# Recurrence of a hybrid trunk on one core: solution and transposed values placed beside the products of levels 1 and 2

## The chip, the cores and the metric

The kernel runs on one core of one Trainium2 chip. The metric is the device time of one execution in microseconds; three runs of a kernel are summed up by their median. TensorE is called PE here, its weight loads PEld, VectorE DVE and ScalarE ACT. PSUM is used as eight banks of 128 partitions by 512 float32 values, `bank0` to `bank7`.

## The reference, cut to what matters

The kernel computes two layers of a trunk over 256 tokens and 256 context tokens: a token mixer (windowed attention, a bidirectional RWKV-7 recurrence, differential attention), then a dense feed-forward layer or a mixture of experts. The change touches the recurrence alone, which a scan defines, per head, over a state of 64 by 64:

```python
def rwkv_scan(s0, r, w, k, v, a_vec, b_vec, reverse, emit):
    def step(s, inp):
        r_t, w_t, k_t, v_t, a_t, b_t = inp
        sa = jnp.einsum('bhvk,bhk->bhv', s, a_t)
        s = s * w_t[:, :, None, :] + sa[..., None] * b_t[:, :, None, :] + v_t[..., None] * k_t[:, :, None, :]
        y = jnp.einsum('bhvk,bhk->bhv', s, r_t) if emit else None
        return s, y
...
    for d, reverse in enumerate((False, True)):
        w_c, k_c, a_c = dirs_c[d]
        s_ctx, y_c = rwkv_scan(s0, r_c, w_c, k_c, v_c, -kk_c, kk_c * a_c, reverse, need_ctx)
        w_l, k_l, a_l = dirs_l[d]
        _, y_l = rwkv_scan(s_ctx, r_l, w_l, k_l, v_l, -kk_l, kk_l * a_l, reverse, True)
```

There are 8 heads of 64 values, two directions and 512 steps (context, then tokens). In layer 1 the context's outputs are not needed (`need_ctx` is false there).

## The kernel before

The 512 steps of a layer are worked off in 8 chunks (`NCH`) of 64 steps. Within a chunk all 64 steps are solved together: a triangular 64 by 64 system for each of 16 head-directions, named by `q` (0 to 7) and `h` (0 or 1, the upper or lower half of the partitions). A step on all sixteen is sixteen small products of 64 by 64 (`pair(x, q, h)` cuts the block out of a 128 by 512 tile). The product's rows are those of the operands' partitions, its columns those of the output's partitions, so one product uses a quarter of the array.

The inverse of the triangular matrix is doubled in five rounds, n = 0 to 4:

- `level(i, n)` multiplies the strictly lower part with the inverse so far, sixteen products into `level_bank` (bank 6). DVE multiplies them by a mask into `T1` (`masked`, L2437, one instruction of 128x512).
- `inverse_doubled(i, n)` waits for `T1` and makes both the grown inverse (`grown`, bank 0) and its transpose (`grown_turned`, bank 1), 32 products, for n = 4 the transpose alone. ACT copies the two banks to `X[1]` and `XT[1]` (`copied`, L1627); the next level waits for the first copy.

Around these stand, in chunk i: `from_state(i)` (the right-hand side: L923 and L927 from the state, then `narrow`, L818), `solve(i - 1)` (the solution U of the chunk before, banks 2 and 7, partitions 0 to 63), `y_of_chunk` and `state` (both L818, both read the copied solution and the kept products), `values_turned(i)` (the values transposed by an identity, banks 2 and 7, partitions 64 to 127), `bonus` (one product of 128x512, for i up to 4), and four pairs `against(i, n)` (four products of 64x192 each), which DVE multiplies by a mask into `PB` (`kept`, L2456). `level(i, 3)` and `level(i, 4)` carry another sixteen products each of the next chunk's matrices (`gram`), one for one between their own (`beside`). In layer 1 no output is made for chunks 0 to 3, so `y_of_chunk` is empty there.

Each engine works off its own list in the order of the code; nothing is scheduled. Lists meet in semaphores: `A` (banks read by ACT), `V_` (banks 3 to 5, read by DVE, claimed in turn), `S` (banks 6 and 7, read by DVE). `pe.wait_ge(A.free, ...)` waits until ACT has copied a bank out, `pe.wait_ge(S.free, ...)` until DVE has masked it. A `V_` claim waits until DVE is through with the bank claimed three claims earlier.

The order of PE in a chunk i from 1 on is: level 0, solve, doubled 0, y, level 1, state, doubled 1, values, bonus, level 2, against 0, doubled 2, against 2, level 3 with gram, against 4, doubled 3, against 6, level 4 with gram, from_state, doubled 4. DVE's list in the same chunk: masked 0, `rates_in` and `operands` of chunk i + 1 (L2402 to L2413), masked 1, `emitted` (L2464), `responses` (L2418), `state` (L2470 to L2480), `bonus_out` (L2367), masked 2, kept 0 and 1, `centre` (L2389), `bonus_keys` (L2354 and L2355, for i under 4), kept 2 and 3, masked 3, kept 4 and 5, `begin_inverse` (L2441), kept 6 and 7, masked 4, `begin_turned` (L2446, L2448), `bonus_in` (L2361, L2362).

## Time and profile before

| | |
|---|---|
| median of 3 runs | 2892.83 us (2891.24 to 2895.13) |
| profiled execution, its own time | 2893.22 us |
| its span (first to last instruction) | 2891.4 us |
| PE busy | 2797.3 us, 97% of the span, 29030 matmul records |
| DVE busy | 1185.1 us, 41% |
| ACT busy | 683.0 us, 24% |
| recurrence of layer 0, chunk 0 level 3 to the last chunk | 177.1 to 343.1 us |
| recurrence of layer 1, the same | 1440.3 to 1603.3 us |
| mean granted PE clock | 0.991 |

A float32 product shows as two matmul records and two weight loads, so that sixteen products are written x32. In the timeline a row's second number runs from its first start to the modelled end of its last matmul. In a dense run the next step starts a little before that end; the distance from start to start is what a step takes. The two stretches of the recurrence are 329 us of the 2891.

### The profile page before, as it was taken

The numbers are of one execution on the slowest core, as the hardware profiler recorded it, in microseconds if no ns is written. First come the engines' busy times: TensorE is split into PE (matmuls) and PEld (weight loads), VectorE is DVE, ScalarE is ACT, GpSimd is POOL, SyncE is SP. The second block draws the span as 40 slices with busy tenths as digits, with TensorE's granted clock in tenths as the row PEclk, the third lists the DMA queues.
The fourth block names the chain that finished last, engine by engine and source line by source line (L and its number), as shares of the span: only waits on it lengthen the run. The fifth ranks groups of instructions, "written<-read, shape, count | busy, mean of one in ns | idle before, by whom it ended". The sixth has DMA issues, their size and how long they took to land.

```text
span 2891.4 us, 63725 instructions
## 1 busy us (share of the span) xinstructions
PE 2797.3 (97%) x29030; PEld 1683.3 (58%) x29030; DVE 1185.1 (41%) x2444; ACT 683.0 (24%) x1425; POOL 3.0 (0%) x7
## 2 busy tenths in 40 slices
PE   7999999999999999999999999989999999999997
PEld 4478777445777888864588787863333333333332
DVE  4777565445545444247786564431111011011101
ACT  2345312544322111013454126520000000000000
POOL 0000000000000000000000000000000000000000
PEclk9999999999999999999999999999999999999999
DMA  7100143212242433232000442459999999999995
...
DMA packets 188787, 534.55 MB, mean 185 GB/s; under 512 B 6113, under 2 KB 80097, under 8 KB 171105
## 3 DMA queue, kind: packets, MB, share of 16 engines
...
## 4 chain that ended last, share of the span: by engine, by line
PE 92%; DVE 4%; ACT 1%; SPq 1%; issue 1%; DMA 1%; DVEq 0%; ACTq 0%
PE bank L572 68%; PE bank L700 12%; PE bank L1337 8%; PE bank L818 2%; PE bank L1199 1%; SPq L2990 1%; DVE WR L2456 1%; ACT ar L1627 0%; DMA rep<-in_repeated 0%; PE bank L923 0%; ACT WR L1627 0%; DVE RS L2330 0%; DVE AT L2127 0%; DVE ar L2389 0%; DVE WR L2437 0%
## 5 line engine op out<-in xcount | busy, mean ns | idle before, releaser
L572 PE MATMUL bank<-AT,WR 128*128 128x512 f32 (+1 forms) x1408 | 521.4, 521 | 5.9 <-ACT AT L1627 3.7
L1627 ACT ACTIVATE ar<-bank 128x256 f32<-128x256 f32 (+2 forms) x338 | 155.1, 463 | 1535.3 <-PE bank L572 1028.3
L572 PE MATMUL bank<-WR,ar 128*32 128x512 f32 (+1 forms) x4464 | 444.5, 555 | 1.6 <-DVE ar L2899 1.6
L572 PE MATMUL bank<-ar 128*32 128x512 f32 (+6 forms) x3990 | 429.6, 509 | 9.9 <-ACT ar L1627 5.9
L572 PEld LDWEIGHTS bank<-AT,WR 128*128 128x128 f32 x1408 | 263.0, 192 | 213.0 <-issue 196.9
L572 PEld LDWEIGHTS bank<-ar 128*32 128x32 f32 (+3 forms) x3990 | 176.1, 124 | 248.5 <-issue 237.3
L572 PEld LDWEIGHTS bank<-WR,ar 128*32 128x32 f32 x4464 | 143.7, 110 | 288.4 <-issue 285.8
L1627 ACT ACTIVATE WR<-bank 128x512 f32<-128x512 f32 (+1 forms) x224 | 122.8, 592 | 200.0 <-PE bank L572 174.7
L572 PE MATMUL bank<-AT,ar 128*32 128x512 f32 (+1 forms) x1456 | 151.5, 561 | 11.3 <-ACT AT L1627 11.3
L2909 DVE TENSOR_TENSOR YB<-YB,bank 128x512 f32<-128x512 f32 x28 | 18.0, 684 | 342.9 <-PE bank L572 342.9
L2917 DVE TENSOR_TENSOR ar<-ar,bank 128x512 f32<-128x512 f32 (+1 forms) x48 | 29.8, 621 | 286.9 <-PE bank L572 285.5
L1627 ACT ACT_TABLE_LOAD x111 | 142.4, 1283 | 14.3 <-DVE ar L2291 8.5
L572 PE MATMUL bank<-WR 64*64 64x64 f32 x5120 | 113.7, 221 | 3.7 <-issue 1.7
L572 PEld LDWEIGHTS bank<-WR 64*64 64x64 f32 x5120 | 100.7, 134 | 18.4 <-DVE WR L2437 7.9
L572 PEld LDWEIGHTS bank<-AT,ar 128*32 128x32 f32 x1456 | 47.8, 110 | 105.8 <-issue 103.6
L572 PE MATMUL bank<-WR,HT 64*64 64x64 f32 x2560 | 94.7, 221 | 5.6 <-ACT WR L1627 3.1
L572 PEld LDWEIGHTS bank<-WR,HT 64*64 64x64 f32 x2560 | 82.7, 134 | 26.5 <-ACT WR L1627 16.7
L2437 DVE TENSOR_TENSOR WR<-bank,tab 128x512 f32<-128x512 f32 x80 | 55.2, 690 | 60.0 <-PE bank L572 58.4
L1627 ACT ACTIVATE ar<-ar 128x256 f32<-128x256 f32 (+2 forms) x137 | 54.1, 446 | 103.3 <-DVE ar L2839 35.3
L1337 PE MATMUL bank<-AT,WR 128*128 128x256 f32 x320 | 76.1, 381 | 0.0
L700 PE MATMUL bank<-ar,WR 128*128 128x256 f32 x336 | 75.0, 379 | 0.6 <-issue 0.6
L700 PE MATMUL bank<-ar 128*128 128x256 f32 x328 | 73.1, 379 | 0.0
...
## 6 DMA issues: line engine op xcount, KB each, us to landing
...
```

What stands on the lines that cost most here:

```text
L572: return pe.matmul(o, lhsT, rhs, start=first, stop=last)
L700: last = pe.matmul(out, one, two, start=not opened and k == 0, stop=k == h.K - 1, skip_group_check=opened)
L818: last = pe.matmul(pair(bank, q, 1 - h if crossed else h), lhs(q, h), rhs(q, h), start=not (opened or (more and q)), stop=not more, skip_g ...
L1199: last = pe.transpose(bank[:, 128 * b:128 * b + 128], Pb[:, n % 2, c, 128 * b:128 * b + 128], eye)
L1337: last = pe.matmul(out, lhs(k), rhs(k), start=not opened and k == 0, stop=k == 3, skip_group_check=opened)
L1627: return act.activation(out, in_, func, **k)
L2437: TT(dq(T1), step_product(banks[6]), mk(M_LEVEL + 1 + n), ALU.mult).then_inc(S.free, 1)
L2456: TT(PB[:, q:q + 2, h, :], bank[:, 0:384].rearrange("p (q w) -> p q w", q=2), stacked[:, q // 4, :].unsqueeze(1).to_broadcast([128, 2, 192 ...
L2909: TT(x, x, b3, ALU.add).then_inc(S.free, 1)
L2917: TT(x, x, bank[:, 0:WIDE[s_]], ALU.mult).then_inc(up.free, 1)
L2990: sp.dma_start(tab[:, TAB_FIRST:], io["tables"][:, TAB_FIRST:]).then_inc(tables_in, 16)
```

## The change

What it does, by engine:

- PE: `solve(i - 1)` is no longer a step of its own; its sixteen products are placed between those of `level(i, 1)`. `values_turned(i)` is likewise placed between those of `level(i, 2)`. `y_of_chunk(i - 1)` and `state(i - 1)` stand behind `inverse_doubled(i, 1)`. `inverse_doubled(i, 2)` stands ahead of `against(i, 0)`, and each further pair of `against` one place later, the last one between level 4 and `from_state`. The number of products is the same.
- PSUM: the level's product, the grown inverse and its transpose take turns over banks 0, 1 and 6 (`level_bank`, `grown_bank`, `turned_bank`); the solution lies in bank 2 and the transposed values in bank 7, each over all 128 partitions. From this come new waits: level 0 for the copy of the right-hand side (`G`), doubled 0 for the copy of the last transpose (`XT`, which for n = 4 goes to a third tile), `from_state` for the copy of `XT` of round 3.
- ACT: the solution is copied behind the two copies of round 0 instead of ahead of them; the two copies of a pair wait once.
- DVE: `responses` and `centre` stand behind masked 1, `emitted` ahead of masked 2, `state` and `bonus_out` behind masked 2, `kept` one place later each, the last pair behind masked 4, and `bonus_keys` behind kept 4 and 5, ahead of masked 4.

The mask is one 128x512 instruction for each level, as before.

The diff, cut to its core:

```diff
+        def level_bank(i, n):
+            return banks[(0, 1, 6)[(5 * i + n + 1) % 3]]
+        def grown_bank(i, n):
+            return banks[(0, 1, 6)[(5 * i + n + 2) % 3]]
+        def turned_bank(i, n):
+            return banks[(0, 1, 6)[(5 * i + n) % 3]]
+        solved_bank, gram_bank = banks[2], banks[7]
...
-                grown, grown_turned, level_bank, gram_bank = banks[0], banks[1], banks[6], banks[7]
-                two = (banks[2], banks[7])
...
+                def value_turned(i, q, h):
+                    c = CH * (i if q < 4 else BWD[i])
+                    last = mm(pair(gram_bank, q, h), Rv[64 * h:64 * h + 64, q % 4, c:c + CH],
+                              eye[64 * h:64 * h + 64, 64 * h:64 * h + 64], True, True)
...
+                def solve(i, q, h):
+                    last = mm(pair(solved_bank, q, 1 - h), pair(XT[2], q, 1 - h), pair(G, q, 1 - h), True, True)
...
                     for q in range(8):
+                        bank = level_bank(i, n)
                         for h in range(2):
...
+                        for h in range(2 if beside else 0):
+                            if beside == "solve":
+                                solve(i - 1, q, h)
+                            elif beside == "values":
+                                value_turned(i, q, h)
...
                     if i:
                         level(i, 0)
-                        solve(i - 1)
                         inverse_doubled(i, 0)
+                        level(i, 1, "solve")
+                        inverse_doubled(i, 1)
                         y_of_chunk(i - 1, ybank)
-                        level(i, 1)
                         state(i - 1)
-                        inverse_doubled(i, 1)
-                        values_turned(i)
+                        level(i, 2, "values")
                         if i <= 4:
                             bonus(i - 1)
-                        level(i, 2)
+                        inverse_doubled(i, 2)
                         pe.wait_ge(responses_ready, seen(responses_ready))
                         against(i, 0)
-                        inverse_doubled(i, 2)
-                        against(i, 2)
                     level(i, 3, "X" if i < NCH - 1 else None)
-                    against(i, 4)
+                    against(i, 2 if i else 4)
                     inverse_doubled(i, 3)
-                    against(i, 6)
+                    against(i, 4 if i else 6)
                     level(i, 4, "LT" if i < NCH - 1 else None)
-                    if i == 0:
+                    if i:
+                        against(i, 6)
+                    else:
                         pe.wait_ge(uv_cleared, seen(uv_cleared))
                     ybank = from_state(i)
                     inverse_doubled(i, 4)
```

On PE, in chunk 1 of layer 0, these rows stood ahead of the change (`WR,HT` is a level's product, `WR` alone a doubling or the solution, L818 the `narrow` steps, `tab,ar` the values, `ar,tab` the bonus, `HT,RS 128x192` an `against`):

```order
L572 MATMUL bank<-WR,HT 64x64 x16
L572 MATMUL bank<-WR 64x64 x48
L818 MATMUL bank<-WR 64x64 x16
L572 MATMUL bank<-WR,HT 64x64 x16
L818 MATMUL bank<-WR 64x64 x16
L572 MATMUL bank<-WR 64x64 x32
L572 MATMUL bank<-tab,ar 64x64 x16
L572 MATMUL bank<-ar,tab 128x512
L572 MATMUL bank<-WR,HT 64x64 x16
L572 MATMUL bank<-HT,RS 128x192 x4
L572 MATMUL bank<-WR 64x64 x32
L572 MATMUL bank<-HT,RS 128x192 x4
```

With the change the same place reads (L583 is L572 there, L829 is L818; the pairs of x2 rows go on eight times each):

```order
L583 MATMUL bank<-WR,HT 64x64 x16
L583 MATMUL bank<-WR 64x64 x32
L583 MATMUL bank<-WR,HT 64x64 x2
L583 MATMUL bank<-WR 64x64 x2
...
L583 MATMUL bank<-WR 64x64 x34
L829 MATMUL bank<-WR 64x64 x32
L583 MATMUL bank<-WR,HT 64x64 x2
L583 MATMUL bank<-tab,ar 64x64 x2
...
L583 MATMUL bank<-ar,tab 128x512
L583 MATMUL bank<-WR 64x64 x32
L583 MATMUL bank<-HT,RS 128x192 x4
```

The solution and the values have no rows of sixteen of their own any more. Behind level 0 stands doubled 0 at once, behind it level 1, and behind that doubled 1; the two L818 steps are together; level 2 is followed by the bonus alone.

On DVE, in chunk 1 of layer 0, from masked 2 to masked 4 (L2437 the mask, L2456 `kept`, L2354 and L2355 `bonus_keys`):

```order
L2437 TENSOR_TENSOR WR<-bank,tab 128x512
L2456 TENSOR_TENSOR WR<-bank,tab 128x2x192 x2
L2389 TENSOR_TENSOR ar<-ar 128x520
L2354 TENSOR_TENSOR ar<-ar 128x512
L2355 TENSOR_SCALAR ar<-ar,vec,cvec 128x512
L2456 TENSOR_TENSOR WR<-bank,tab 128x2x192 x2
L2437 TENSOR_TENSOR WR<-bank,tab 128x512
L2456 TENSOR_TENSOR WR<-bank,tab 128x2x192 x2
L2441 COPY_PREDICATED WR<-tab,bank 128x512
L2456 TENSOR_TENSOR WR<-bank,tab 128x2x192 x2
L2437 TENSOR_TENSOR WR<-bank,tab 128x512
```

With the change (L2455 is the mask, L2474 `kept`, L2372 and L2373 `bonus_keys`), from masked 3 on:

```order
L2455 TENSOR_TENSOR WR<-bank,tab 128x512
L2474 TENSOR_TENSOR WR<-bank,tab 128x2x192 x2
L2459 COPY_PREDICATED WR<-tab,bank 128x512
L2474 TENSOR_TENSOR WR<-bank,tab 128x2x192 x2
L2372 TENSOR_TENSOR ar<-ar 128x512
L2373 TENSOR_SCALAR ar<-ar,vec,cvec 128x512
L2455 TENSOR_TENSOR WR<-bank,tab 128x512
L2474 TENSOR_TENSOR WR<-bank,tab 128x2x192 x2
L2464 COPY_PREDICATED HT<-tab,bank 128x512
```

The two instructions of `bonus_keys` moved from ahead of masked 3 to ahead of masked 4, and the last pair of `kept` moved behind masked 4.

## Rows read from the trace of the kernel before

**Rows 1.** The page: busy time, share of the span and instructions

```profile
PE 2797.3 (97%) x29030; PEld 1683.3 (58%) x29030; DVE 1185.1 (41%) x2444; ACT 683.0 (24%) x1425; POOL 3.0 (0%) x7
```

**Rows 2.** Busy us by stretch, both recurrences: PE, PEld, DVE, ACT, POOL, PE clock, DMA

```profile
177.08:343.09 166.01, 157.94 (x5528) 138.45 (x5526) 120.50 (x212) 82.67 (x204) 0.00 (x0) 1.00 0.02 5
1440.33:1603.30 162.97, 152.03 (x5304) 134.13 (x5302) 117.91 (x204) 82.53 (x204) 0.00 (x0) 1.00 0.02 4
```

**Rows 3.** Timeline of PE, chunk 1 of layer 0: start, length, instruction

```profile
183.65 0.97 PE L572 MATMUL bank<-WR,HT 64*64 64x64 f32 x26
...
184.59 2.33 PE L572 MATMUL bank<-WR 64*64 64x64 f32 x94
186.85 1.15 PE L818 MATMUL bank<-WR 128*64 128x64 f32 x32
```

**Rows 4.** Timeline of PE, chunk 4 of layer 0, values and bonus to level 3

```profile
262.84 1.10 PE L572 MATMUL bank<-tab,ar 64*64 64x64 f32 x32
263.87 1.12 PE L572 MATMUL bank<-ar,tab 128*128 128x512 f32 x2
...
268.81 0.27 PE L572 MATMUL bank<-WR,HT 64*64 64x64 f32 x2
...
269.90 0.92 PE L572 MATMUL bank<-HT,ar 64*128 64x192 f32 x8
```

**Rows 5.** Timeline of PE, chunk 2 of layer 0, level 2 to against 4

```profile
217.82 1.15 PE L572 MATMUL bank<-WR,HT 64*64 64x64 f32 x32
218.90 0.92 PE L572 MATMUL bank<-HT,ar 64*128 64x192 f32 x8
219.76 1.16 PE L572 MATMUL bank<-WR 64*64 64x64 f32 x64
220.85 0.92 PE L572 MATMUL bank<-HT,ar 64*128 64x192 f32 x8
...
223.28 0.92 PE L572 MATMUL bank<-HT,ar 64*128 64x192 f32 x8 [0.41 <-DVE WR L2456]
```

**Rows 6.** Timeline of DVE over the same stretch

```profile
219.01 0.69 DVE L2437 TENSOR_TENSOR WR<-bank,tab 128x512 f32<-128x512 f32 x1 [0.40 <-PE bank L572]
...
221.40 0.68 DVE L2354 TENSOR_TENSOR ar<-ar 128x512 f32<-128x512 f32 x1
222.12 0.55 DVE L2355 TENSOR_SCALAR ar<-ar,vec,cvec 128x512 f32<-128x512 f32 x1
222.58 1.02 DVE L2456 TENSOR_TENSOR WR<-bank,tab 128x384 f32<-128x384 f32 x2
```

**Rows 7.** Timeline of PE, chunk 3 of layer 1, where y is empty

```profile
1495.22 1.15 PE L572 MATMUL bank<-WR,HT 64*64 64x64 f32 x32 [0.78 <-ACT WR L1627]
1496.30 1.15 PE L818 MATMUL bank<-WR 128*64 128x64 f32 x32
```

**Rows 8.** Who waited for whom: PE, layer 0, us in total, times, longest

```profile
PE bank L572 <- issue: 2.4, 7, 0.4
PE bank L927 <- issue: 1.7, 3, 0.7
...
PE bank L818 <- issue: 1.0, 2, 0.7
PE bank L923 <- issue: 0.3, 1, 0.3
PE bank L818 <- ACT WR L1627: 0.2, 1, 0.2
```

**Rows 9.** The same, layer 1

```profile
PE bank L572 <- issue: 4.0, 9, 0.9
...
PE bank L818 <- issue: 2.2, 3, 1.1
```

**Rows 10.** Busy time by stretch, from one issue gap of PE to the next

```profile
212.24:215.98 3.74, 3.31 (x128) 3.04 (x127) 2.82 (x7) 0.73 (x2) 0.00 (x0) 1.00 0.03 7
235.88:239.61 3.73, 3.36 (x127) 3.09 (x128) 2.57 (x6) 0.44 (x1) 0.00 (x0) 1.00 0.02 4
```

145 lines of the change are left out of this document (78 added, 67 removed).

## The prediction

> **What bounds the kernel now.** I read the page's busy shares first: TensorE is busy for 2797.3 of 2891.4 us, VectorE for 41% and ScalarE for 24% [rows 1]. So only what lengthens or shortens TensorE's own list counts. The change touches two stretches, so the busy time by stretch comes next [rows 2]: 166.01 us in layer 0 and 162.97 us in layer 1, with PE busy for 157.94 and 152.03 us. DVE and ACT have a quarter and half of the time free there, and the granted clock is 1.00, its upper level. The stretches hold seven chunks with changed order each, and chunk 0, which keeps its order. Then the timelines of PE and DVE, for one thing: how long a step of sixteen products takes, and what covers the time between a product and the step that needs it masked or copied. Last the waits, for what is idle on PE already: mostly "issue", a wait that no other engine ends [rows 8, 9].
>
> Steps, from start to start. A level alone takes 1495.22 to 1496.30, 1.08 us [rows 7]; y and state have as many products and I give them the same. Level 0, solution and doubled 0 take 183.65 to 186.85, 3.20 us, of which a doubling is 1.09 (219.76 to 220.85), so that level 0 and solution have about 1.05 each [rows 3, 5]. The values take 262.84 to 263.87, 1.03, and I count 1.0 since the last of them runs into the bonus [rows 4]. Thirty-two products placed one for one, level 3 with gram, take 268.81 to 269.90, 1.09 us, no more than sixteen alone [rows 4]. An against takes 218.90 to 219.76, 0.86 us [rows 5].
>
> **What goes.** In each of 14 chunks the solution's 1.05 and the values' 1.0, together 2.05 us, since level 1 with the solution and level 2 with the values should take the 1.09 of level 3 with gram: each uses the same two quarters of the array beside the level's two. That is 28.7 us off PE's list. Of PE's order it is the only gain; no DMA is issued in the moved steps, and no queue of SP or POOL is passed.
>
> **What it uncovers.** Those steps were cover.
> (a) Doubled 0 now stands right behind level 0. A level started at 217.82, its mask on DVE ran from 219.01 for 0.69 us, the doubling started at 219.76 [rows 5, 6]: 1.94 us after the level's start, of which the level's step is 1.08. Idle: 0.86 us.
> (b) Level 1 stands right behind doubled 0 and needs the copy of the grown inverse. In layer 1, chunks 1 to 4, y is empty and this wait is there today: 0.78 us by the row [rows 7], 0.85 from start to start. Idle: 0.85 us, but new only in the ten chunks that had y there.
> (c) Doubled 1 stands right behind level 1, where the state step was: 0.86 us. `operands` and `rates_in` stand ahead of this mask on DVE; they take some 3.1 us behind masked 0, and level 1 now ends 3.1 us after masked 0's end too, so I add nothing.
> (d) Doubled 2 stands behind the bonus (1.05 us, cover enough) in chunks 1 to 4, and bare in chunks 5 to 7: 0.86 us there. Its old cover, against 0, now covers the copy ahead of level 3, which needs 0.85 of its 0.86.
> (e) The last `kept` pair stands behind masked 4, and `narrow` in `from_state` waits for it. From the end of level 4: against 6 (0.86) and the state part (0.97) give PE 1.83 us; DVE begins the pair when against 6 is over and takes 1.02 for it [rows 6], so it is ready at about 2.05. Idle 0.2 us in chunks 4 to 7. In chunks 1 to 3 `bonus_keys` (0.68 and 0.55, 1.2 together [rows 6]) stand ahead of masked 4 and start only behind kept 4 and 5; mask and last pair come about 0.9 later: 1.1 us.
> (f) Given back: today `bonus_keys` delay kept 2 and 3, and against 4 waits for a bank, idle 0.41 [rows 5], 0.62 more than a normal start; it starts behind doubled 3 now. Minus 0.62 in chunks 1 to 3. y's wait for the copied solution, 0.2 us once by its row [rows 8] and some hundredths elsewhere, goes: minus 0.1 in the ten chunks with y.
> (g) The rotated banks: level 0 waits for the copy of G, which has all of doubled 4 (1.08) for some 0.8; doubled 0 for the last XT, which has level 0. Nothing, while doubled 4 stands there; bare it would be 0.8. State and bonus_out on DVE run later, but their readers, `from_state` and against 2, are over 1 us away: nothing. The copy of U stands behind two copies on ACT and y comes a doubling later: nothing.
>
> The sum per chunk. Layer 0, chunks 1 to 3: -2.05 + 0.86 + 0.85 + 0.86 + 1.1 - 0.62 - 0.1 = +0.9, three times 2.7. Chunk 4: -2.05 + 2.57 + 0.2 - 0.1 = +0.6. Chunks 5 to 7: 0.86 more, +1.5, three times 4.5. Layer 1, chunks 1 to 3: -2.05 + 1.72 + 1.1 - 0.62 = +0.15, together 0.45. Chunk 4: -0.1. Chunks 5 to 7: 4.5. In all +12.6 us: by waits alone the change is a loss.
>
> **What the idle time is worth.** PE is short of instructions in the same stretches. Its issue waits are 2.4 + 1.7 + 1.0 + 0.3 = 5.4 us in 13 pieces in layer 0 and 4.0 + 2.2 = 6.2 us in 12 pieces in layer 1 [rows 8, 9]. Idle time is counted from the end of the last matmul, some 0.22 us behind its start, and a normal start follows after 0.03, so each piece costs 0.19 more: 11.6 + 25 x 0.19 = 16.4 us. From one such gap to the next lie 256 records (128 matmuls and 127 or 128 loads) and 3.7 us [rows 10]. I read this as a fetch of 256 instructions that takes about 3.65 us, begun when the one before is begun upon. In layer 0 there are 5528 + 5526 records, 43 blocks, 3.84 us each, 3.64 without the idle pieces: right at that bound. The new order spreads the same records over more time, so waits for a mask and for a fetch fall together. Where can fetches still bind? From level 1 to the end of doubled 2: 128 + 128 + 64 + 64 + 4 + 128 + 128 = 644 records, 2.5 blocks, 9.1 us, in 1.95 + 1.09 + 1.08 + 1.08 + 1.09 + 1.05 + 1.09 = 8.4 us. Up to 0.7 us a chunk is lost there, and I take 0.57, since a block seldom begins just there: 14 times, 8.0 us. Elsewhere a chunk has 14 us for 900 records, which need 12.8. So 16.4 - 8.0 = 8.4 us come back. Bounds: nothing, or all 16.4.
>
> Net +12.6 - 8.4 = +4.2 us on the profiled execution's 2893.22, of which the span is 2891.4. It lies 0.4 us above the median of 2892.83, so I put the median at 2897.
>
> A rule of the Trainium skill speaks against the paired steps. The rows have 64 matmul records in 1.09 us, 17 ns each [rows 4]. "TensorE: Matmul & The Clock Gate", section "Wait — 56ns, not 53.3ns?", says that starts never follow closer than about 25 ns, however small the product; by it an estimate of a paired step is 64 x 25 ns = 1.6 us, and the sum would be 28 x 0.5 = 14 us worse. The trace does not agree: in separate quarters of the array starts are 17 ns apart. By the row it is +4.2, by the rule +18.
>
> **The rivals.**
> 1. The issue waits stay as they are (slower). Mechanism: gaps fall at fixed counts of instructions, and if these counts fall inside the dense run level 1 to doubled 2, a gap there delays mask and copy with it and nothing is absorbed. For it: today's gaps sit in runs just as dense. Against it: 3.84 us a block becomes about 3.9, above the 3.65. Price: +12.6, 2905.4. It decides from the point where less than 6.8 of the 16.4 come back. Chance 0.26.
> 2. The waits overlap more than I sum (faster). The last `kept` pair has work ahead of it on PE; if `narrow` never waits, (e) falls away, 6 x 1.1 + 8 x 0.2 = 8.2 us, and with 13 of the 16.4 back it is +12.6 - 8.2 - 13 = -8.6, 2884. For it: DVE is idle for a quarter of the stretch. Against it: masked 4 cannot be earlier than level 4, and the pair is behind it. Chance 0.14.
> 3. The paired steps cost more than 1.09, because the solution reads two tiles that ACT wrote last or because of their starts: 28 x 0.5 = +14 us on +4.2, 2911. Against it: all of today's pairs are at 1.09 [rows 4]. Chance 0.03.
>
> **How the numbers follow.** Forecast, a loss in waits mostly paid by fetches that are hidden: 0.57, 2897, its own range 2890 to 2901. Rival 1 0.26, rival 2 0.14, rival 3 0.03. A difference of 0.2%, 5.8 us, is about what a measurement of this kernel can tell from no change: same means 2887.0 to 2898.6. Of the forecast's 0.57 some 0.07 lies over 2898.6; of rival 1 0.05 and of rival 2 0.04 lie within. Same 0.59, slower 0.31, faster 0.10. The range reaches from 2887 to 2906: it leaves out rival 3, the rest of rival 1 above its price, and most of rival 2.
>
> **What would show it.** In the changed profile, both stretches a little longer, near 168 and 165 us. PE waits for DVE's mask (L2455) ahead of doubled 0 and doubled 1, 28 times some 0.6 to 0.7 by the rows, and in six chunks ahead of doubled 2; for ACT's copy ahead of level 1 in all 14; for `kept` (L2474) ahead of `narrow`, near 0.9 in the six chunks with `bonus_keys`. Paired steps at 1.09. PE's issue waits down from 11.6 to about 5 us. The forecast is wrong if issue waits stay near 11 (then rival 1), if the waits for `kept` are missing (rival 2), or if the median moves without these stretches moving: a longer list of instructions that shifts fetch gaps elsewhere.

## The result, and the profile after

| | before | after |
|---|---|---|
| median | 2892.71 us (2891.24 to 2895.13) | 2919.03 us (2917.68 to 2922.07) |
| profiled execution, its own time | 2893.22 us | 2918.77 us |
| its span | 2891.4 us | 2916.9 us |

The ratio is 1.0091, with a 95% interval of 1.0078 to 1.0103: slower by 26 us, clear of the noise, and outside the predicted range of 2887 to 2906. The direction of the net forecast (+4.2) was right, the size was not.

Where did it come from? The stretches are cut here from the mask of chunk 0, level 3, to the last mask of chunk 7. Busy time by stretch; the columns are those of [rows 2]. Before:

```profile
177.08:340.01 162.93, 154.86 (x5418) 135.61 (x5420) 119.81 (x212) 82.08 (x203) 0.00 (x0) 1.00 0.02 5
1440.33:1600.29 159.96, 149.02 (x5194) 131.36 (x5196) 117.22 (x204) 81.93 (x203) 0.00 (x0) 1.00 0.02 4
```

And after:

```profile
175.77:352.41 176.64, 150.33 (x5394) 130.59 (x5394) 119.12 (x209) 83.81 (x203) 0.00 (x0) 0.94 0.02 4
1452.71:1624.57 171.86, 139.62 (x5170) 120.27 (x5169) 116.09 (x201) 83.81 (x203) 0.00 (x0) 0.99 0.02 4
```

The two stretches grew from 322.89 to 348.50 us, by 25.6; the span grew by 25.5. So all of it lies here. PE is busy for 14 us less and idle for 40 us more, and in layer 0 the granted clock is 0.94 where it was 1.00. What PE waited for, us in total, times, longest, in layer 0 (against [rows 8]):

```profile
PE bank L583 <- DVE WR L2455: 12.9, 15, 1.1
PE bank L583 <- ACT WR L1644: 6.3, 9, 0.8
PE bank L583 <- issue: 4.8, 8, 1.0
PE bank L583 <- DVE WR L2474: 0.7, 1, 0.7
PE bank L951 <- issue: 0.5, 1, 0.5
PE bank L829 <- DVE WR L2474: 0.5, 1, 0.5
PE bank L947 <- issue: 0.4, 1, 0.4
PE bank L829 <- issue: 0.3, 1, 0.3
```

In layer 1 (against [rows 9]):

```profile
PE bank L583 <- DVE WR L2455: 15.1, 17, 1.0
PE bank L583 <- issue: 8.4, 10, 1.5
PE bank L583 <- ACT WR L1644: 4.7, 7, 0.7
PE bank L829 <- DVE WR L2474: 1.6, 3, 0.6
```

L2455 is the mask, L1644 the copy, L2474 `kept`. The waits for masks and copies are there, 32 and 16 of them. The issue waits are there too, 6.0 us in layer 0; they were to fall by half. How the front of a chunk looks now, PE in chunk 1 of layer 0 (start, length, instruction, idle time before it), against [rows 3]:

```profile
184.60 1.16 PE L583 MATMUL bank<-WR 64*64 64x64 f32 x64 [1.06 <-DVE WR L2455]
186.44 0.27 PE L583 MATMUL bank<-WR,HT 64*64 64x64 f32 x2 [0.67 <-ACT WR L1644]
...
189.20 1.99 PE L583 MATMUL bank<-WR 64*64 64x64 f32 x64 [0.85 <-DVE WR L2455]
191.12 3.11 PE L829 MATMUL bank<-WR 128*64 128x64 f32 x64
194.15 0.27 PE L583 MATMUL bank<-WR,HT 64*64 64x64 f32 x2
...
195.24 1.12 PE L583 MATMUL bank<-ar,tab 128*128 128x512 f32 x2
```

Doubled 0 waits for its mask, level 1 for its copy, doubled 1 for its mask, as (a) to (c) said. Level 2 with the values takes 1.09 us (194.15 to 195.24). Doubled 1 shows something that no step of the prediction had: it takes 1.92 us from start to start (189.20 to 191.12), where a doubling takes 1.09 by [rows 5]. The stretches of lower clock, busy time by stretch, PE's clock third from the end:

```profile
186.58:193.41 6.83, 5.98 (x171) 5.70 (x169) 3.18 (x5) 2.56 (x5) 0.00 (x0) 0.50 0.01 2
265.09:268.50 3.41, 3.19 (x88) 3.10 (x90) 1.29 (x3) 1.76 (x4) 0.00 (x0) 0.50 0.02 5
288.98:295.81 6.83, 5.97 (x150) 5.68 (x142) 2.65 (x5) 2.27 (x4) 0.00 (x0) 0.50 0.02 5
316.29:319.70 3.41, 3.41 (x92) 3.29 (x86) 0.19 (x2) 1.19 (x3) 0.00 (x0) 0.50 0.02 5
1466.58:1470.00 3.42, 3.04 (x86) 2.96 (x87) 1.44 (x3) 1.84 (x4) 0.00 (x0) 0.50 0.02 5
```

For 23.9 us the granted clock was 0.50, its lower level, 1.2 GHz. Before, the clock stood at 1.00 in both stretches. Ahead of the first of these stretches PE had waited 1.06 us for a mask and then 0.67 for a copy.

**The account.** I add up, over both stretches, the distances from the start of one matmul to the start of the next, by what the second one waited for. "Running" is all the rest.

| us | before | after | difference | predicted |
|---|---|---|---|---|
| running | 296.8 | 273.9 | -22.9 | -28.7 |
| waits for DVE | 3.8 (6) | 39.2 (37) | +35.4 | +33.7 |
| waits for ACT | 4.3 (5) | 14.5 (16) | +10.2 | +7.5 |
| issue waits | 17.9 (26) | 20.7 (24) | +2.8 | -8.4 |
| sum | 322.8 | 348.3 | +25.5 | +4.1 |

In brackets are the times. The predicted entries are the prediction's own: 34 masks at 0.86, (e) 8.2, (f) -3.7; ten copies at 0.85, less 1.0. Of "running" after, 548 matmuls started at the lower clock, in 20.8 us, 38 ns each. With 24.5 ns as the usual distance that is 7.5 us extra, an estimate; taken pair by pair of the same shapes at the upper level it is 8.6. Without the 7.5 running fell by 30.4. So 18.7 of the 21 us by which the sum missed are two lines: issue waits that rose by 2.8 instead of falling by 8.4 (11.2 us), and the lower clock, which had no term (7.5).

### The profile page after: what moved, and what is told of

Read it like the earlier page. It is cut to its first block, busy times and chain, and to the rows that moved or that the text cites. A ratio compares the mean times of both kernels' runs of the same rounds, so it can differ in the third digit from the quotient of the medians.

```text
span 2916.9 us, 63772 instructions
## 1 busy us (share of the span) xinstructions
PE 2783.2 (95%) x29030; PEld 1668.1 (57%) x29030; DVE 1185.0 (41%) x2444; ACT 686.7 (24%) x1425; POOL 3.0 (0%) x7
## 4 chain that ended last, share of the span: by engine, by line
PE 92%; DVE 5%; ACT 1%; issue 1%; DMA 1%; SPq 0%; DVEq 0%; ACTq 0%
PE bank L583 68%; PE bank L711 12%; PE bank L1354 8%; PE bank L829 2%; PE bank L1216 1%; DVE WR L2455 1%; DMA WR<-in_low_first 1%; ACT WR L1644 0%; ACT ar L1644 0%; DVE WR L2474 0%; PE bank L947 0%; DVE RS L2348 0%; DVE AT L2145 0%; DVE HT L2137 0%; DVE AT L2132 0%
## 5 line engine op out<-in xcount | busy, mean ns | idle before, releaser
L583 PE MATMUL bank<-AT,WR 128*128 128x512 f32 (+1 forms) x1408 | 519.1, 519 | 6.0 <-ACT AT L1644 3.7
L1644 ACT ACTIVATE ar<-bank 128x256 f32<-128x256 f32 (+2 forms) x338 | 155.1, 463 | 1535.1 <-PE bank L583 1028.1
L583 PE MATMUL bank<-WR,ar 128*32 128x512 f32 (+1 forms) x4464 | 444.5, 555 | 1.6 <-DVE ar L2929 1.6
L583 PE MATMUL bank<-ar 128*32 128x512 f32 (+6 forms) x3990 | 429.7, 509 | 9.4 <-ACT ar L1644 5.4
L583 PEld LDWEIGHTS bank<-AT,WR 128*128 128x128 f32 x1408 | 262.1, 191 | 211.6 <-issue 197.2
L583 PEld LDWEIGHTS bank<-ar 128*32 128x32 f32 (+3 forms) x3990 | 176.2, 124 | 248.0 <-issue 236.8
L583 PEld LDWEIGHTS bank<-WR,ar 128*32 128x32 f32 x4464 | 143.8, 110 | 288.3 <-issue 285.7
L1644 ACT ACTIVATE WR<-bank 128x512 f32<-128x512 f32 (+1 forms) x224 | 126.4, 594 | 223.0 <-PE bank L583 178.7
L583 PE MATMUL bank<-AT,ar 128*32 128x512 f32 (+1 forms) x1456 | 151.7, 562 | 12.2 <-ACT AT L1644 12.2
L583 PE MATMUL bank<-WR 64*64 64x64 f32 x5120 | 118.9, 227 | 34.5 <-DVE WR L2455 28.0
L583 PEld LDWEIGHTS bank<-WR 64*64 64x64 f32 x5120 | 105.5, 140 | 53.0 <-ACT WR L1644 26.1
L583 PE MATMUL bank<-WR,HT 64*64 64x64 f32 x2560 | 96.8, 223 | 17.3 <-ACT WR L1644 9.4
L583 PEld LDWEIGHTS bank<-AT,ar 128*32 128x32 f32 x1456 | 47.8, 110 | 106.7 <-issue 104.5
L583 PEld LDWEIGHTS bank<-WR,HT 64*64 64x64 f32 x2560 | 84.0, 136 | 34.0 <-ACT WR L1644 18.3
L2455 DVE TENSOR_TENSOR WR<-bank,tab 128x512 f32<-128x512 f32 x80 | 55.2, 690 | 71.3 <-PE bank L583 69.5
L1644 ACT ACTIVATE ar<-ar 128x256 f32<-128x256 f32 (+2 forms) x137 | 54.1, 447 | 102.9 <-DVE ar L2869 35.3
L2474 DVE TENSOR_TENSOR WR<-bank,tab 128x384 f32<-128x384 f32 x128 | 65.2, 550 | 21.7 <-PE bank L583 21.4
## 6 DMA issues: line engine op xcount, KB each, us to landing
WR<-in_moe_w_down SPq DMA_DIRECT2D x27, 2048.0 KB, 15.1
WR<-in_moe_w_up SPq DMA_DIRECT2D x15, 2048.0 KB, 15.8
```

The lines of the kernel that those rows point to most:

```text
L583: return pe.matmul(o, lhsT, rhs, start=first, stop=last)
L1644: return act.activation(out, in_, func, **k)
L2455: TT(dq(T1), step_product(level_bank(i, n)), mk(M_LEVEL + 1 + n), ALU.mult).then_inc(S.free, 1)
L2474: TT(PB[:, q:q + 2, h, :], bank[:, 0:384].rearrange("p (q w) -> p q w", q=2), stacked[:, q // 4, :].unsqueeze(1).to_broadcast([128, 2, 192 ...
```

## The experiments

Four questions: are the waits as large as summed; what is each part worth alone; are issue waits and the lower clock two costs or one; and why were the waits not absorbed. The same account of every kernel, both stretches, in us. "Lower clock" is the running time spent at 0.50, of which some third is loss. "Late" counts instruction packets, explained with the last question, in 80 to 84 blocks a kernel.

| kernel | ratio, 95% | stretches | running | DVE | ACT | issue | lower clock | late, of them behind a mask |
|---|---|---|---|---|---|---|---|---|
| before | 1 | 322.9 | 296.8 | 3.8 | 4.3 | 17.9 | 0 | 1, 0 |
| after | 1.0091 (1.0078 to 1.0103) | 348.5 | 273.9 | 39.2 | 14.5 | 20.7 | 20.8 | 19, 15 |
| a2 | 1.0090 (1.0065 to 1.0116) | 347.8 | 269.2 | 41.7 | 14.5 | 22.1 | 12.4 | 18, 16 |
| e1 | 1.0075 (1.0058 to 1.0091) | 337.7 | 316.6 | 5.1 | 0 | 15.8 | 0 | 11, 7 |
| e2 | 1.0094 (1.0076 to 1.0111) | 345.3 | 281.1 | 39.3 | 2.0 | 22.5 | 0 | 13, 9 |
| e9 | 1.0099 (1.0083 to 1.0114) | 349.3 | 278.8 | 38.5 | 6.8 | 24.9 | 6.9 | 12, 10 |
| e11 | 1.0108 (1.0093 to 1.0123) | 346.1 | 263.5 | 41.2 | 12.5 | 28.1 | 0 | 19, 17 |
| e6 | 1.0095 (1.0069 to 1.0122) | 346.7 | 274.2 | 40.4 | 14.9 | 16.8 | 23.8 | 16, 13 |
| e3 | 1.0055 (1.0038 to 1.0072) | 334.4 | 263.8 | 41.0 | 12.4 | 16.9 | 0 | 13, 12 |
| e5 | 1.0062 (1.0042 to 1.0082) | 340.6 | 281.1 | 24.4 | 12.6 | 22.4 | 0 | 15, 10 |
| e14 | 1.0071 (1.0058 to 1.0085) | 345.4 | 290.2 | 25.1 | 11.7 | 18.2 | 0 | 12, 8 |
| e16 | 1.0112 (1.0096 to 1.0127) | 356.8 | 265.0 | 43.1 | 15.6 | 33.2 | 8.6 | 22, 15 |
| e17 | 1.0048 (1.0034 to 1.0062) | 334.4 | 293.9 | 10.1 | 5.8 | 24.4 | 0 | 10, 8 |
| e4 | 0.9990 (0.9978 to 1.0002) | 315.0 | 285.0 | 3.6 | 9.6 | 16.8 | 0 | 3, 0 |
| e7 | 0.9997 (0.9985 to 1.0008) | 318.9 | 286.2 | 3.6 | 9.5 | 19.2 | 0 | 4, 0 |
| e8 | 0.9970 (0.9958 to 0.9981) | 314.9 | 283.9 | 3.8 | 9.2 | 18.0 | 0 | 5, 0 |
| e10 | 1.0040 (1.0026 to 1.0053) | 332.6 | 309.6 | 3.8 | 4.0 | 15.1 | 0 | 2, 0 |
| e12 | 1.0001 (0.9992 to 1.0010) | 323.4 | 294.3 | 3.8 | 12.4 | 12.9 | 0 | 0, 0 |
| e13 | 1.0027 (1.0017 to 1.0036) | 331.1 | 291.5 | 17.9 | 12.4 | 9.2 | 0 | 1, 0 |
| e15 | 0.9991 (0.9982 to 1.0000) | 321.6 | 275.4 | 24.3 | 12.4 | 9.3 | 0 | 1, 0 |

### The changed kernel again, and its waits filled

a2 is the changed kernel itself, beside the runs of its batch:

> The changed kernel once more, for a second profile and a time beside the others. All theories: 2916 to 2920. Clock theory: half-clock stretches of some 20 us again. If the half clock comes and goes between executions of this kernel, the profile shows clearly more or less than the 24 us of the first, and the two sums of the stretches differ by several us.

Measured: ratio 1.009, the same. Its lower clock holds for 12.4 us of running and not 20.8, its issue waits are 1.4 longer, and the stretches differ by 0.7 us. That is a hint, no more, that the two lines trade against each other.

e1 puts a product of 128 by 384 that nothing reads at each bared place (e2 has the same `fill`):

```diff
+                def fill(bank):
+                    mm(bank[:, 0:384], blk, tb("masks")[:, 0:384], True, True)
...
                         level(i, 0)
+                        fill(banks[2])
                         inverse_doubled(i, 0)
+                        fill(banks[2])
                         level(i, 1, "solve")
+                        fill(banks[7])
                         inverse_doubled(i, 1)
...
                             bonus(i - 1)
+                        else:
+                            fill(banks[2])
                         inverse_doubled(i, 2)
```

> The changed kernel with one product of 128x384 by constants, result unused (0.79 us by the 1.05 us of the bonus's 128x512), into a free bank in each wait that the change uncovered: behind level 0, behind doubled 0, behind level 1, and behind level 2 in chunks 5 to 7. No dependency is shortened. Clock theory (the bunched idle pieces of 0.9 us bring PE to half its clock, about 24 us of the two recurrences, worth some 10 us): the stretches at 0.50 vanish and the time falls by about 10 us, to 2909. Run-ahead theory (issue waits grow because PE stops at waits, 15.4 us against 11.6 before): issue waits fall back to 11 too, 4 to 6 us more, 2903 to 2905. Waits-alone theory (everything lost is the latency of masks and copies): 2919 or a little more, since the same waits are only filled.

Measured: 2912.88 against 2889.82. The waits for masks and copies are gone, the lower clock too, the issue waits are 2.1 under before's. The time lies between the clock theory's 2909 and the 2919 of waits alone. What is left over before in the stretches is 14.8 us: running is 19.8 longer, the waits for ACT and the issue waits are shorter. The 48 fillers take 1.03 us each from start to start, not the 0.79 that I had planned, about as much as the waits they replace. That is near the size of the waits by the sum, +12.6. So a kernel with this cover and without the lower clock is at what "by waits alone the change is a loss" gave, with almost nothing absorbed. Another 5 us of its profiled span lie outside the stretches, where nothing was changed; no row here explains them.

### Are the lower clock and the issue waits two costs?

e2 fills the one wait ahead of level 1, e9 does so with a product half as wide, and e11 puts 32 products of 64 by 64 once ahead of each layer's chunks, so that every later instruction stands 128 records further on. The edit of e2 and e9, then that of e11:

```diff
                         inverse_doubled(i, 0)
+                        fill(banks[2])
                         level(i, 1, "solve")
```

```diff
+                for n in range(2):
+                    for q, h in hq:
+                        mm(pair(solved_bank, q, h), eye[64 * h:64 * h + 64, 64 * h:64 * h + 64],
+                           eye[64 * h:64 * h + 64, 64 * h:64 * h + 64], True, True)
                 ybank = None
```

> The changed kernel with that filler behind doubled 0 alone, so that the two idle pieces in front of doubled 0 and doubled 1 stay. Clock theory: with the middle of the three pieces filled the half-clock stretches are rare, some 6 to 10 us gained, 2909 to 2913. Run-ahead theory alone: PE still stops at 31 waits for masks, so little is gained, under 3 us. Waits-alone theory: no change, 2919.

> The changed kernel with one product of 128x192 by constants behind doubled 0 alone, short enough (some 0.4 us by the 1.05 of 128x512) that level 1 waits for its copy as before. Clock theory: half-clock stretches are gone, and since nothing else is longer now, the sum of both stretches falls by what the records at half clock cost, 548 records at 38 ns instead of 24.5, 7.5 us from the first profile, 4.7 from the second: 341 to 343 us for both, median about 2913. If half-clock stretches stay, one idle piece less is not enough and nothing is gained. If they go and the time stays, other waits take their place.

> The changed kernel with 32 products of 64 by 64 by constants, results unused, once ahead of chunk 0's level 3 in each layer: 128 records, half a block, 2.2 us of PE a layer. The ends of the blocks of 256 then fall half a block later within each chunk. If the late fetches hang on where a block ends relative to the waits for masks, issue waits (20.7 us from start to start in both stretches) move by 5 us or more, either way, in at least one layer. If they hang on the number of instructions alone: within 3 us of 20.7, and the time 4 us over the changed kernel's.

Measured: 2918.54, 2919.96 and 2922.76. In e2 and e11 the lower clock is gone from the stretches and in e9 a third of it is left, yet none is faster. In e9 and e11 what went at the clock came back as issue waits, 24.9 and 28.1 us against 20.7; in e2 only 1.8 of the 7.5 did (22.5). The sum of issue waits and the loss at the lower clock is 28.2 after, 26.8 in a2, 22.5 in e2, 27.6 in e9 (2.6 of it clock) and 28.1 in e11. Layer 1 of e9, what PE waited for:

```profile
PE bank L583 <- DVE WR L2459: 14.3, 16, 1.0
PE bank L583 <- issue: 8.1, 13, 1.3
PE bank L583 <- ACT WR L1648: 1.6, 6, 0.8
```

I read this as one cost and not two: with the array at half speed for a while the next instructions are there in time, and where it runs at full speed PE waits for them. For the theory that the clock cost the 7.5 us, e9 is a miss (341 to 343 us expected in the stretches, 349.3 measured), e2 is one too by its time, and e11 speaks against it. The sum isn't a constant, though: it is 5.7 lower in e2, and in e16, below, some 8 higher. The line to explain is "short of instructions", 28 us after against 17.9 before. e11 says one thing more: half a block of extra records moved the issue waits by 7.4 us, so they hang on where the blocks end, as its expectation had it.

### The parts alone

e4 is the kernel before with the values beside level 2 and nothing else moved; e7 also moves `bonus_keys` behind `begin_turned`; e8 is e4 with most of the values left out, as its expectation says. The core of e4's edit:

```diff
-                        values_turned(i)
                         if i <= 4:
                             bonus(i - 1)
-                        level(i, 2)
+                        level(i, 2, "values")
```

> The kernel before with one part of the change alone: the values are placed between the products of level 2, in bank 7, and the bonus stands ahead of level 2; solution, y, state, against and DVE's list as before. By waits: minus 1.0 us in chunks 1 to 4 of both layers (the bonus covers the copy ahead of level 2), minus 0.15 in chunks 5 to 7, 9 us less than before, 2884. If instruction delivery gives half of it back: 2888. If any uncovered wait costs the clock: chunks 5 to 7 show stretches at 0.50 and the time is 2893 or more.

> The kernel before with the values beside level 2 and with bonus_keys behind begin_turned. Against the version with the values alone (which was at 0.999 of the kernel before): the wait of against 4, 0.62 us in six chunks, goes, 3.7 us; if instruction delivery takes half of it back, 2 us. Against the kernel before: 0.9975 to 0.998. The PE waits for kept (1.2 us in each layer before) are gone.

> The version of the kernel before with the values beside level 2, and 14 of these 16 products left out in chunks 1 to 7 (the values of the chunks are wrong therefore); they took no time of their own. The same leaving out took 14 us off the two stretches in the changed kernel (348.2 to 334.4), where PE stops at masks. If the time of 256 instructions binds everywhere at 3.65 us: 3.06 blocks, 11 us less, 2876 to 2878. If it binds only where PE stops at waits (run-ahead theory): clearly less here than there, 3 to 5 us, 2883 to 2885. If a record costs nothing here: 2887.

Measured: 2887.3 (0.999), 2891.75 (0.9997) and 2886.05 (0.997, against 2892.86). e4 saves 11.8 us of running, gives 5.3 back to copies and nothing to masks: 7.9 us less in its stretches, of which the median shows about 3. It is the step that keeps its cover. e7 is a miss: its stretches are 3.9 us longer than e4's. The waits for `kept` are gone, as expected, but three waits for a mask, 3.0 us, have come in their place, and the issue waits are 2.4 longer. e8 shows what the rest of the values cost in their place beside level 2: nothing in the stretches. The paired step is as cheap as [rows 4] have it.

e3 leaves most of the values out of the changed kernel, e5 takes the solution out of level 1 and puts it back behind level 0, e14 undoes the second pairing as well. The edit of e5:

```diff
                         level(i, 0)
+                        pe.wait_ge(A.free, A.jobs[("XT", l, i - 1, 4)])
+                        for q, h in hq:
+                            solve(i - 1, q, h)
                         inverse_doubled(i, 0)
-                        level(i, 1, "solve")
+                        level(i, 1)
```

> The changed kernel with 14 of the 16 products that transpose the values left out in chunks 1 to 7 (the values of the chunks are wrong therefore). They are paired with a level's products and take no time of their own: level 2 with them 1.09 us, alone 1.08. If instruction delivery does not bind, the time stays at 2919. If PE is bound by the delivery of 256 instructions in 3.65 us, 56 records less in 14 chunks are 3.06 blocks, 11 us less, 2908. If it binds in part, as I put it in the prediction, 3 to 6 us less.

> The changed kernel with the solution as a step of its own again, between level 0 and doubled 0; everything else as changed (y and state behind doubled 1, values paired). By the waits alone: 1.05 us of step comes back for 0.86 us of wait, 14 times 0.19, 3 us slower than the changed kernel. Run-ahead theory: PE stops one time less per chunk and its queue stays filled, so that issue waits (15.4 us in the changed kernel) fall by about a third and no half clock shows, since the three idle pieces in a row are two: 3 to 8 us faster than the changed kernel.

> The changed kernel with both pairings undone: the solution between level 0 and doubled 0, the values between state and level 2; banks, y, state, against and DVE's list as changed. Steps: 28.7 us back; the mask ahead of doubled 0 is covered again, 14 times 0.95 = 13.3 us; +15 us against the changed kernel if fetches stay as late. If pairing is what makes the fetches late and brings the half clock (28 us of issue and half clock there, 9 us in the version with two idle pieces and no pairing), 19 us come back: -4 us, 2915, with no stretch at 0.50 and hardly a fetch that starts over 1.9 us after its block. If the places are the cause: 2930 and over.

Measured: 2907.45, 2913.55 and 2914.96. In e3 the stretches are 14 us shorter, although the DVE and ACT waits together are within 0.4 us of after: running fell by 10.1, of which 7.5 is the lower clock that is gone, and issue waits by 3.8. In e8 the same omission brought nothing. Fewer records help where PE is short of them. e5 shows the first pairing by itself: with the solution apart, running is 7.2 longer, DVE waits are 14.8 shorter, the lower clock is gone, and the kernel is 6 us faster than the changed kernel beside it (2913.55 against 2919.11). **Pairing the solution with level 1 is a loss**, where (a) had a gain of 0.19 us a chunk. Without the lower clock the pairing saves 14.7 us of running and bares 14.8 of waits for DVE, nothing in sum; the loss is the shortage of instructions (28.2 against 22.4) and 1.9 of ACT. e14 is the more telling one. It has no paired step that was not there before, and its issue waits are still 18.2, with 25.1 us of DVE waits beside them. Its time is what its expectation gave if pairing were the cause (2915), but the sign that was to go with it, hardly a late packet, is missing: there are 12.

e6 moves `bonus_keys` behind `begin_turned` in chunks 1 to 3, to take (e) away:

```diff
                         kept(i, 4, 6)
-                        if i < 4:
-                            bonus_keys(l, i)
...
+                    if 0 < i < 4:
+                        bonus_keys(l, i)
```

> The changed kernel with bonus_keys of chunks 1 to 3 moved on DVE behind begin_turned, where nothing waits for it. By my term for the last kept pair: 6 times 0.9 = 5 us faster than the changed kernel. By the waits for kept in the profile of the changed kernel (0.5 in layer 0, 2.5 in layer 1): 3 us faster, and these waits gone.

Measured: 2920.02, nothing gained, a miss. DVE waits rose by 1.2. The waits that this was to remove had been small: ahead of `narrow` (L829) the changed kernel waited for `kept` four times, 2.1 us in total by the rows above, not six times 1.1. In e6 1.1 of it is left, and the waits for masks rose from 28.0 to 31.1 us by the rows, the longest from 1.1 to 1.7: `bonus_keys` now stand ahead of the next chunk's mask.

e10 is the kernel before with the values as eight products of 128 columns:

```diff
-                    for q, h in hq:
+                    for q in range(8):
...
-                        last = mm(two[h][64:128, 64 * q:64 * q + 64], ...
+                        last = mm(two[q // 4][64:128, 128 * (q % 4):128 * (q % 4) + 128], Rv[:, q % 4, c:c + CH], eye,
```

> The kernel before, and only the transposing of the values written otherwise: eight products of 128 rows by 128 columns instead of sixteen of 64 by 64, into the same two banks. By columns streamed the step takes the same 1.0 to 1.08 us; PE gets 32 records less in 14 chunks, 448, 1.75 blocks of 256. If instruction delivery binds at 3.65 us a block: 6.4 us faster, 0.9978. If it binds in part: 2 to 4 us, 0.999. If only PE's own time counts: 1.0.

Measured: 2902.43, slower. The records are halved, but the step takes 1.96 us where sixteen small ones take 1.03. The last nine of its sixteen matmuls and the bonus behind them, PE in chunk 1 of layer 0:

```profile
189.84 1.15 PE L572 MATMUL bank<-tab,ar 128*64 128x128 f32 x9
190.91 1.13 PE L572 MATMUL bank<-ar,tab 128*128 128x512 f32 x2
```

That is 119 ns a matmul. I had taken the step as unchanged; 14 times 0.93 is 13 us, and running rose by 12.8. With fewer records over more time the issue waits fell by 2.8.

### Are waits absorbed at all?

The step "what the idle time is worth" says that a wait for another engine takes the place of a fetch. e12 and e13 test it in the kernel before, with no pairing and the banks as they were: y behind level 1, so that level 1 stands bare of cover for the copy; then y and state both behind doubled 1, so that the mask is bare too. e15 adds the values beside level 2 to e13. The edit of e13:

```diff
                         inverse_doubled(i, 0)
-                        y_of_chunk(i - 1, ybank)
                         level(i, 1)
+                        inverse_doubled(i, 1)
+                        y_of_chunk(i - 1, ybank)
                         state(i - 1)
-                        inverse_doubled(i, 1)
```

> The kernel before with y moved from ahead of level 1 to behind it; nothing paired, no instruction more or less. Level 1 then waits for the copy of the grown inverse in the ten chunks that have y: 0.98 us from start to start by the rows of layer 1, less 0.1 of a normal start, 0.85 to 0.9 us, 9 us in all. If idle pieces are paid in full: +9 us, 1.003. If the fetch of instructions runs in them (my prediction's step): issue waits, 17.9 us from start to start before, fall by 4 and the sum is +5, 1.0015. If an idle piece makes the next fetch late: issue waits rise and it is over +9.

> The kernel before with y and state both behind doubled 1. Besides the copy ahead of level 1 (9 us) doubled 1 waits for its mask in 14 chunks, 0.95 us each, 13 us; y's and state's work stands ahead of the values then and covers nothing that needs it. In full: +22 us, 1.0077. With fetches absorbed as in my prediction: +13. If late fetches come on top: +25 or more. Half-clock stretches would show that two idle pieces of 0.9 us on either side of a level are enough to lower the granted clock; in the changed kernel there were three.

> The kernel before with y and state behind doubled 1 (1.0027 of the kernel before) and, in addition, the values beside level 2. The step of the values goes, 14 us. If pairing spoils the absorption: issue waits rise from 9 us to 18 or more and the net is -5 us, 1.001. If pairing does no harm by itself: -12 to -14 us, 0.998.

Measured: 2895.42 (1.0001), 2902.67 (1.0027) and 2893.11 (0.9991). What PE waited for in e13, layer 0:

```profile
PE bank L572 <- DVE WR L2437: 5.6, 7, 0.8
PE bank L572 <- ACT WR L1627: 4.8, 7, 0.7
PE bank L572 <- DVE WR L2456: 1.9, 4, 0.7
PE bank L927 <- issue: 1.7, 4, 0.5
PE bank L923 <- issue: 0.7, 2, 0.4
PE bank L572 <- issue: 0.5, 2, 0.3
```

In e12 8.1 us of new waits for ACT cost nothing: issue waits fell from 17.9 to 12.9, and small gaps shrank by the rest. In e13 22.2 us of new waits cost 8.2, and issue waits fell to 9.2. So the mechanism is real, and it is as large as I had it: 8.7 us of 17.9 (8.4 of 16.4 in the prediction). e15 is e13 with the values beside level 2; it takes 9.5 us off e13's stretches, gives 6.4 of DVE waits for it, and keeps the issue waits at 9.3. What absorbed the waits in these kernels does not do so in the changed one.

### Why not in the changed kernel

The trace has the instruction packets, 16 KB each, one for 256 of PE's records. In every kernel, where PE stands for one, it starts again 1.35 to 1.41 us on average after the packet's end (1.19 to 1.61 for a single one). The packet itself comes some 1.1 to 1.2 us behind the first record of the block before, by the median, and takes about 1.1. That makes the 3.7 us of [rows 10]. The first block of [rows 10], cut just ahead of its packet's start (the last two columns are the DMA engines' busy share and GB/s):

```profile
212.24:213.39 1.15, 1.15 (x35) 1.08 (x36) 0.30 (x1) 0.00 (x0) 0.00 (x0) 1.00 0.00 0
213.39:215.98 2.59, 2.17 (x101) 1.96 (x97) 2.52 (x7) 0.73 (x2) 0.00 (x0) 1.00 0.04 9
```

And two blocks in a row of the changed kernel, chunk 6 of layer 1, cut in the same way:

```profile
1589.78:1592.20 2.42, 1.63 (x100) 1.52 (x91) 1.72 (x4) 1.18 (x2) 0.00 (x0) 1.00 0.00 0
1592.20:1593.60 1.40, 1.40 (x49) 1.11 (x42) 0.73 (x2) 1.08 (x2) 0.00 (x0) 1.00 0.06 12
1594.85:1597.35 2.50, 2.50 (x104) 2.21 (x108) 1.51 (x3) 0.00 (x0) 0.00 (x0) 1.00 0.00 0
1597.35:1598.80 1.45, 1.45 (x37) 1.05 (x27) 1.15 (x3) 1.09 (x2) 0.00 (x0) 1.00 0.04 11
```

Each packet starts 2.5 us behind the block's first record, not 1.15. PE over the same time:

```profile
1591.25 1.16 PE L583 MATMUL bank<-WR 64*64 64x64 f32 x64 [0.79 <-DVE WR L2455]
1592.34 0.92 PE L583 MATMUL bank<-HT,ar 64*128 64x192 f32 x8
...
1594.85 0.27 PE L583 MATMUL bank<-RS,HT 64*64 64x64 f32 x2 [0.98 <-issue]
...
1596.45 1.16 PE L583 MATMUL bank<-WR 64*64 64x64 f32 x64
1597.54 0.92 PE L583 MATMUL bank<-HT,ar 64*128 64x192 f32 x8
...
1599.75 0.27 PE L583 MATMUL bank<-WR,HT 64*64 64x64 f32 x1 [0.92 <-issue]
```

One wait for a mask ahead of doubled 2, and then 0.98 and 0.92 of issue waits: the blocks take 5.07 and 4.90 us. Both packets start some 1.0 us behind the start of a doubling. Counted over both stretches, with "late" for a packet over 1.9 us behind its block: before has 1 of 84, the changed kernel 19 of 83, and 15 of these 19 start 1.0 to 1.3 us behind the end of a mask (of the other 64 only 5 do). The mask need not leave PE idle for it: in e1 nearly no wait is left, and 7 of its 11 late packets stand there. I read this as a fetch that is asked for only once PE's list is past the doubling's wait for its mask. Then a wait ahead of that point adds to the 3.7 us of the block, and only a wait behind it is absorbed. The table's last column sorts the kernels: 7 to 17 such packets in each with the new order, none in before, e4, e7, e8, e10, e12, e13 and e15.

e16 and e17 were to find the part of the change that does it. e16 puts the second half of the chunk back as it was, `kept` and `bonus_keys` with it; e17 has the new second half, but no pairing, and y and state in their old places. Both keep the banks in turn with their waits and DVE's new order in the first half. The edit of e16 on PE:

```diff
-                        inverse_doubled(i, 2)
                         pe.wait_ge(responses_ready, seen(responses_ready))
                         against(i, 0)
+                        inverse_doubled(i, 2)
+                        against(i, 2)
                     level(i, 3, "X" if i < NCH - 1 else None)
-                    against(i, 2 if i else 4)
+                    against(i, 4)
                     inverse_doubled(i, 3)
-                    against(i, 4 if i else 6)
+                    against(i, 6)
                     level(i, 4, "LT" if i < NCH - 1 else None)
```

> The changed kernel with the second half of the chunk as it was before: against 0 ahead of doubled 2, each further pair one place earlier, `kept` and `bonus_keys` in the old order; the paired steps, the bank rotation and the waits of the first half stay. Theory (instruction fetches are begun late because of the second half's new places): e13_both_later and e14_unpaired differ by 14.3 us in the stretches although only this half and the banks differ, 7 us of it in waits and 9 in issue waits (9.2 to 18.2). So here the stretches fall by about 14 us from 348.5 to about 334, issue and half clock together from 28 to some 18 us, packets that start more than 1.9 us behind their block from 17 to a few; the kernel near 2905. Rival (the paired steps and bare masks of the first half make the fetches late): issue and half clock stay near 27, only the waits of the second half go, 6 to 7 us; the kernel near 2912.

> The kernel before with the second half of the change alone (and the bank rotation): doubled 2 ahead of against 0, the further pairs one place later with their `kept`; solution, y, state and values stand apart, y and state where they were. Theory (the second half makes the fetches late): 322.9 us in the stretches, plus some 6.5 us of waits, plus 9 us of issue waits, about 338; the kernel near 2908. Rival (the first half does): the waits are partly covered by the issue waits of before (17.9 falls to some 14), so about 326; the kernel near 2896.

Measured: 2924.59 and 2904.41. e16 speaks against the theory that the second half alone is the cause: with it undone the issue waits rose to 33.2 us, and 15 late packets stand behind a mask. What PE waited for in its layer 1:

```profile
PE bank L583 <- DVE WR L2454: 11.7, 13, 1.0
PE bank L583 <- issue: 9.5, 14, 1.3
PE bank L583 <- ACT WR L1643: 5.5, 8, 0.8
PE bank L829 <- issue: 5.4, 4, 1.7
```

e17, with the second half alone, lies between the two forecasts, 11.5 us over before, nearer to the theory's 15: 7.8 of it waits, and 6.5 issue waits that rose where the rival had them fall.

So neither half is the cause by itself. What after, e16, e17 and e14 share, and e13 and e15 lack, are three things: the banks in turn with their new waits for copies, DVE's new order of `responses`, `centre`, `emitted` and `state`, and a third that the description of the change leaves out. e15 and e16 differ by these, and by the solution beside level 1, and by 35 us: 18.8 of DVE waits, 3.2 of ACT and 23.9 of issue waits against 10.4 of running.

The third is two lines of `inverse_doubled` that changed places:

```diff
                 def inverse_doubled(i, n):
-                    pe.wait_ge(S.free, S.jobs[("T1", l, i, n)])
                     if n:
                         pe.wait_ge(A.free, A.jobs[("XT", l, i, n - 1)])
...
+                    pe.wait_ge(S.free, S.jobs[("T1", l, i, n)])
```

Of two waits ahead of a product, the one that the code names first is carried by the product's first weight load, and the other becomes an instruction of its own, an `EVENT_SEMAPHORE` in PE's list. Before, that was the wait for the copy of `XT` (L890). With the change it is the wait for the mask (L913). PEldq is PE's list itself; the rows give how often the instruction runs, its length in ns, and its first and last start:

```profile
L890 PEldq EVENT_SEMAPHORE  x64: 51/51/51, 160.6 to 1601.5; - x64
L913 PEldq EVENT_SEMAPHORE  x78: 51/51/51, 161.8 to 1627.2; - x78
```

It is so in every kernel with the new order, and in none of the eight with the old one: PE sat idle for a mask 339 times in all stretches, 299 times with the wait as an instruction of its own (new order) and 40 times with the wait on the weight load (old order). Two things go with it. The doubling starts 0.84 us behind its mask's start in each of the new kernels (e1's two waits aside), and 0.74 or 0.75 in e7, e13 and e15. And the packet of the next block waits too. Among records 8 to 55 of a block of 256, a wait for a mask that is an instruction of its own had the packet start 0.85 to 1.5 us after PE went on in 57 of 61 cases. With the wait on the weight load the packet had started before PE went on in 14 of 14. Within the kernels of the new order the waits of a level for its copy are on the weight load: there, in the same place, 19 of 20 packets had started before PE went on. From record 72 on the kind of wait makes no difference: the packet was there first in 195 of 196 cases and in 25 of 25.

Such a pair. e13, chunk 5 of layer 0: doubled 1 waits at record 29 of its block and goes on at 285.18; the packet (DMA in the second stretch) comes while PE stands.

```profile
283.76:284.89 1.13, 0.63 (x22) 0.49 (x18) 1.13 (x2) 0.00 (x0) 0.00 (x0) 1.00 0.00 0
284.89:285.18 0.29, 0.00 (x0) 0.00 (x0) 0.24 (x1) 0.00 (x0) 0.00 (x0) 1.00 0.30 56
```

After, chunk 4 of layer 0: doubled 0 waits at record 24 and goes on at 260.23; nothing comes until 261.30.

```profile
258.75:261.30 2.55, 1.59 (x82) 1.43 (x78) 1.95 (x4) 0.23 (x1) 0.00 (x0) 1.00 0.00 0
```

So the traces show which waits delay a packet: those that are an instruction of their own and stand in the first 60 or so of the block's 256 records. A chunk is nearly six blocks long, so that a doubling that stands there does so in several chunks in a row (doubled 0 in layer 0 of the changed kernel: records 4, 24, 44 and 59). That points at the swapped waits as what makes the packets late. What isn't shown is how much of the 10.3 us between 17.9 and 28.2 they cost: no kernel was run with the two lines alone in their old order, nor one with the banks in turn alone.

## Why the prediction missed

**What goes, -28.7: right.** Running fell by 22.9, and by 30.4 without the 7.5 us at the lower clock. The paired steps take 1.09 us for 64 matmuls, 17 ns each, where the Trainium skill has about 25 ns from start to start ("TensorE: Matmul & The Clock Gate", section "Wait — 56ns, not 53.3ns?"); this trace does not agree with it. e8 confirms that the values cost nothing in their new place. Rival 3 is out.

**(a), (c), (d), the masks: right place, a tenth too small.** 34 waits at 0.86 were summed; 32 came, 28.0 us in the rows, 0.88 each. With the 0.19 between last start and modelled end each is 1.07 from start to start, of which 0.12 would be a normal start's: 0.95. The mask's start to the doubling's start is 0.84, not the 0.75 of [rows 5, 6]; that tenth goes with the wait that became an instruction of its own.

**(b), the copies: right place, a little too small.** 11.0 us in 16 pieces by the rows; from start to start the line rose by 10.2, where 7.5 was summed.

**(e), `kept` ahead of `narrow`: too large.** 8.2 was summed; four waits came, 2.1 us in the rows, 2.9 from start to start. Its excess made up for what the masks lacked: DVE's line in all is +35.4, predicted +33.7. A sum that comes out right by two errors is luck. Rival 2 rested on this term; it was half right there, but the gain that it had with it did not come.

**"What the idle time is worth", -8.4: the step that failed.** Issue waits rose by 2.8, and another 7.5 us lie at the lower clock in their place. I had modelled a block as 3.65 us from its first record, so that every other wait within it was free. Only the last part of it is so: packet and restart, some 2.5 us from the packet's start in all kernels. Its first part, in the blocks that PE stood for, grew from 1.22 us in layer 0 and 1.57 in layer 1 to 1.98 and 2.17, and these blocks from 3.73 and 4.02 to 4.45 and 4.62 us. The first part grows by a wait that stands early in the block as an instruction of its own, and the change made the wait for the mask such an instruction; (g) went through the new waits and not through their order. In e12 and e13, where packets are on time, the step holds, with the size that I gave it. My rule was right for kernels that I had not been asked about.

**Rival 1** came nearest in what it says, with nothing absorbed: 2905.4 against 2919.0. (Rival 3's 2911 is the nearer number, by luck: its cost did not come.) Its mechanism, gaps that fall into the dense run and delay mask and copy with them, is close to what was found, but it stopped at zero. It had no room for waits that lengthen the fetches. The range shared that: its upper end was all waits and nothing absorbed.

**The lower clock** had no term. [rows 2] have 1.00 in both stretches, and I didn't ask what the new idle pieces would do to it. By e9 and e11 a term for it would have been worth little by itself; by e2 up to 5.7 of the 7.5 us.

No version here beats the kernel before beyond its interval; e4 (0.9990) and e15 (0.9991) come closest, with intervals that end at 1.0002 and 1.0000. e8 is faster, and leaves work out.
